# Two-layer encoder step on one core: the first feed-forward product as seven block products

## The chip, the core and the metric

The kernel runs on one core of one Trainium2 chip. The metric is the device time of one execution in microseconds (us). The five engines are named as the profile names them: PE (TensorE, matrix multiplication), DVE (VectorE), ACT (ScalarE), POOL (GpSimd) and SP (SyncE, which here only issues transfers).

## The reference

Two layers, each a token mixer and then a gated feed-forward part with a causal convolution of width 3. There are 656 token rows: 16 meta rows and 512 prompt rows of one stream, and 8 sample streams of 16 rows. The change touches the feed-forward part only:

```python
def conv_ffn(h, p, buf):
    u = h @ p['w_ffn_up']
    a, v = u[..., :D_FF], u[..., D_FF:]
    T = a.shape[1]
    ext = jnp.concatenate([buf.astype(a.dtype), a], axis=1)
    w = p['ffn_conv_w']
    c = p['ffn_conv_b'] + sum(ext[:, j:j + T] * w[j] for j in range(CONV_W))
    out = (jax.nn.silu(c) * v) @ p['w_ffn_down']
    return out, ext[:, -(CONV_W - 1):]
...
    h = rmsnorm(x, p['norm_ffn_pre'])
    f, buf = conv_ffn(h, p, conv_buf)
    x = x + rmsnorm(f, p['norm_ffn_post'])
```

Here `D_MODEL` = 1024 and `D_FF` = 2816, so `w_ffn_up` is 1024 x 5632 and `w_ffn_down` is 2816 x 1024.

## The kernel before

**Layout.** Everything is feature-major: an activation is 8 tiles of 128 features by `T` = 656 tokens, and a product is taken over two halves of `HALF` = 328 tokens, one half to a PSUM bank. Four PSUM tensors of two banks each (`G0`, `G1`, `WA`, `WB`) hold all products.

**Precision.** A product in float32 is made of three products in the type fp32r: each operand is split in a high part (ACT copies it, which rounds: `whi`, `Hh`, `gh`) and a rest (DVE subtracts: `wlo`, `Hl`, `gl`), and PE takes low x high, high x high and high x low. So a tile of 128 outputs over 8 tiles of inputs is 8 x 2 halves x 3 = 48 matmuls of 128 x 328.

**The stream of weights.** The weights come in pieces of 128 x 1024 through SP into a ring of two raw slots (`wraw`), are split by `w_high` (ACT, line 1156) and `w_low` (DVE, line 1723) into a ring of three slots (`whi`, `wlo`), and PE's `tile` (line 556) waits for the semaphore `w_split` of its piece. ACT waits for the tile that used the slot before.

**The feed-forward part of a layer.** The 22 chunks of 128 gate columns and 128 value columns are worked in two halves of 11. In a half, PE makes for each chunk a gate tile and a value tile (`tile`, called at line 1044 and after), 96 matmuls; then the down product of the half, 8 tiles of 11 chunks, 66 matmuls each. For each chunk DVE takes the gate tile out of PSUM times the norm factor `R` into `ax`, convolves it in three operations into `cc`, ACT takes the silu into `tmp`, DVE multiplies it by `R` and by the value tile, ACT copies the high part into `gh` and DVE subtracts the rest into `gl`. The down product of the first half is copied to `Y` by ACT, that of the second half added to it by DVE. The last three down tiles are worked by halves of the tokens (`last_tiles`, line 601), so that the norm behind them can begin on the first half, and the next layer begins with `first_two` (line 616), three tiles worked by halves as their inputs come.

**What sets the order.** There is no planner: each engine's program is written out by hand, works strictly in order, and waits on counting semaphores. DVE and ACT also wait for their own previous instruction. The helpers through which all instructions pass give their line to the profile: L513 for a matmul, L1642 for DVE, L1082 for ACT; so instructions are told apart by the names of their tiles. POOL's own work (`normalize`, `split_out`, `decay_state`) lies in the token mixer, and POOL has none in the feed-forward part.

## Time and profile before

| | |
|---|---|
| time, median of 3 executions | 1893.23 us (1892.51 to 1893.58) |
| span of the profiled execution | 1891.6 us |
| PE busy | 1851.7 us (98%), 12092 matmuls |
| PE weight loads | 1712.9 us (91%) |
| DVE busy | 1109.8 us (59%), 1803 instructions |
| ACT busy | 753.1 us (40%), 1221 instructions |
| POOL busy | 97.2 us (5%), 105 instructions |
| chain that ended last | PE 85%, DVE 7%, ACT 5% |

The span runs from the first to the last instruction of one profiled execution. No time of its own is given for that execution beside the span: the median of the timed executions lies 1.6 us above it. A busy share says how long an engine worked, not whether anybody waited for it; the chain of work that ended last says that. The granted clock of PE is full (0.9 or more) in each of the 40 slices of the span.

### The profile page before, as it was taken

Reading aid. Unit: us, or ns where it says so; the run is one execution under the profiler, and the core shown is the slowest. Engines: PE = TensorE matmul, PEld = TensorE weight load, DVE = VectorE, ACT = ScalarE, POOL = GpSimd, SP = SyncE. Lnnn points to the kernel's source line nnn. Section 1 sums busy time; section 2 is a strip of 40 time slices with the busy share of each in tenths; the row PEclk is TensorE's granted clock in tenths of the full one; section 3 lists DMA queues with packets and bytes.
Section 4 is the critical chain, followed back from the end, with each engine's and each line's share of the span. In section 5 each row is a group of like instructions: output and inputs, shape, how many; then the busy total and the mean of one; then the engine's idle time right before and its main releaser. Section 6 shows DMA issues by size and latency. Waiting matters only on the chain.

```text
span 1891.6 us, 30407 instructions
## 1 busy us (share of the span) xinstructions
PE 1851.7 (98%) x12092; PEld 1712.9 (91%) x12092; DVE 1109.8 (59%) x1803; ACT 753.1 (40%) x1221; POOL 97.2 (5%) x105
## 2 busy tenths in 40 slices
PE   8999999999999999999999999999999999999996
PEld 7999976598999999999999999657989999999995
DVE  5777875426766226654577778654377551466635
ACT  5444546435422222222564444554363222222234
POOL 0000023200000000000000000340000000000000
PEclk9999999999999999999999999999999999999999
DMA  5312121411222222222231122314112222122211
GB/s 179 95 58 69 63 74 55 158 41 49 80 80 69 78 67 68 79 78 74 65 109 47 58 69 73 80 55 130 56 49 91 77 75 71 67 79 78 68 67 62
DMA packets 46380, 143.83 MB, mean 76 GB/s; under 512 B 5952, under 2 KB 11968, under 8 KB 46216
## 3 DMA queue, kind: packets, MB, share of 16 engines
q1 hardware_dynamic: 38704, 124.12, 20.3%
q10 hardware_dynamic: 7536, 17.78, 2.7%
q8 instruction: 96, 1.57, 0.3%
q14 instruction: 44, 0.36, 0.1%
HBM read 130.80 MB, written 8.65 MB: 74 GB/s over the span
## 4 chain that ended last, share of the span: by engine, by line
PE 85%; DVE 7%; ACT 5%; issue 1%; DMA 1%; ACTq 0%; DVEq 0%; SPq 0%
PE G L513 68%; PE WA L513 10%; PE WB L513 5%; PE G L517 1%; DVE wlo L1642 1%; PE WB L517 1%; ACT sq L1082 1%; DVE DE L1642 1%; ACT R L1082 1%; DVE Z L1642 1%; DVE tmp L1642 1%; ACT Hh L1082 1%; DVE Y L1642 1%; DVE Hl L1642 1%; DMA wraw<-in_wstream 1%
## 5 line engine op out<-in xcount | busy, mean ns | idle before, releaser
L513 PE MATMUL G<-Hh,wlo 128*128 128x328 f32 x2144 | 688.5, 321 | 12.0 <-DVE Hl L1642 8.5
L513 PE MATMUL G<-Hh,whi 128*128 128x328 f32 x2144 | 673.2, 314 | 0.0
L513 PE MATMUL G<-Hl,whi 128*128 128x328 f32 x2144 | 667.8, 311 | 0.0
L513 PEld LDWEIGHTS G<-Hh,wlo 128*128 128x128 f32 x2144 | 404.7, 189 | 23.5 <-DVE Hl L1642 12.6
L513 PEld LDWEIGHTS G<-Hh,whi 128*128 128x128 f32 x2144 | 404.1, 188 | 2.2 <-issue 0.2
L513 PEld LDWEIGHTS G<-Hl,whi 128*128 128x128 f32 x2144 | 404.5, 189 | 0.0
L1082 ACT ACTIVATE whi<-wraw 128x1024 fp32r<-128x1024 f32 (+2 forms) x198 | 203.0, 1025 | 475.8 <-PE G L513 458.0
L1642 DVE TENSOR_TENSOR wlo<-wraw,whi 128x1024 fp32r<-128x1024 f32 (+2 forms) x198 | 234.1, 1182 | 224.7 <-ACT whi L1082 213.6
L513 PE MATMUL G<-gl,whi 128*128 128x328 f32 x628 | 196.6, 313 | 0.0
L513 PE MATMUL G<-gh,wlo 128*128 128x328 f32 x628 | 195.9, 312 | 0.0
L513 PE MATMUL G<-gh,whi 128*128 128x328 f32 x628 | 195.9, 312 | 0.0
L1642 DVE TENSOR_TENSOR ax<-G,R 128x328 f32<-128x328 f32 (+2 forms) x126 | 48.6, 386 | 136.5 <-PE G L513 133.2
L513 PEld LDWEIGHTS G<-gh,whi 128*128 128x128 f32 x628 | 118.0, 188 | 0.0
L513 PEld LDWEIGHTS G<-gh,wlo 128*128 128x128 f32 x628 | 117.9, 188 | 0.0
L513 PEld LDWEIGHTS G<-gl,whi 128*128 128x128 f32 x628 | 117.9, 188 | 0.0
L1082 ACT ACTIVATE tmp<-cc 128x528 f32<-128x528 f32 x88 | 42.1, 479 | 149.2 <-DVE cc L1642 147.8
L1642 DVE SCALAR_TENSOR_TENSOR cc<-ax,cols,cc 128x672 f32<-128x672 f32 x88 | 80.9, 919 | 3.1
L1082 ACT ACTIVATE DE<-DE 128x512 f32<-128x512 f32 (+2 forms) x64 | 43.3, 677 | 63.5 <-DVE DE L1642 59.2
L456 POOL TENSOR_TENSOR S<-S,dec 128x1024 f32<-128x1024 f32 x8 | 15.2, 1898 | 988.4 <-PE WA L513 988.4
L1642 DVE TENSOR_TENSOR DE<-Y 128x328 f32<-128x328 f32 (+4 forms) x128 | 57.9, 452 | 4.8
L513 PEld LDWEIGHTS WA<-Z 128*128 128x128 f32 (+3 forms) x544 | 48.8, 165 | 12.0 <-DVE Z L1642 6.7
L513 PE MATMUL WA<-sq,ones 128*128 128x328 f32 x144 | 52.2, 449 | 4.3 <-ACT sq L1082 4.3
(270 smaller groups left out, 2487.2 us busy)
## 6 DMA issues: line engine op xcount, KB each, us to landing
wraw<-in_wstream SPq DMA_DIRECT2D x192, 512.0 KB, 3.3
ckT<-in_ckT SPq DMA_DIRECT2D x12, 512.0 KB, 3.5
S<-in_s ACTq DMA_DIRECT2D x8, 512.0 KB, 6.1
o_sst<-S ACTq DMA_DIRECT2D x8, 512.0 KB, 2.9
ctok<-in_ctok SPq DMA_DIRECT2D x8, 512.0 KB, 3.6
o_y<-Y SPq DMA_DIRECT2D x16, 164.0 KB, 2.0
ckT<-in_ckT ACTq DMA_DIRECT2D x4, 512.0 KB, 3.9
ctok<-in_ctok ACTq DMA_DIRECT2D x4, 512.0 KB, 4.0
```

Of the source, the lines that this page charges most:

```text
L456: pool.tensor_tensor(s3, s3, dec[:, :].rearrange("p (b a) -> p b a", a=1).broadcast_to([P, DB, P]), ALU.mult).then_inc(S("s0_decayed"), 1)
L513: return pe.matmul(out, lhsT, rhs, start=start, stop=stop, skip_group_check=True)
L517: return pe.transpose(out, in_, ident[0:n, 0:n])
L1082: return act.activation(*args, **kw)
L1642: return kind(*args, **kw)
```

## The change

**Seven products instead of eight.** A chunk is seen as a 2 x 2 by 2 x 2 block product: its weights are four blocks (gate or value columns, first or second half of the 1024 inputs), its inputs four blocks (first or second half of the inputs, first or second half of the tokens). For the chunks 3 to 21 of each layer PE makes seven products of 4 input tiles x 3 = 12 matmuls each, 84 in all, in the order `B11, B21, T2, T3, T1, T4, B22`, in three PSUM banks; results that serve twice are copied or added between the products by ACT and DVE. The chunks 0 to 2 stay as they were ("plain"). PE's program has 9808 rows instead of 10264.

**Sums of inputs and weights.** Per layer POOL makes two differences of token halves, ACT and DVE make sums and their splits from them (`Sh`, `Sl`). Per chunk POOL makes four sums of blocks of weights, 128 x 512 each (`early_sums`: `T3`, `T1`, `T2`; `late_sum`: `T4`), into `t2`, `t3` and in place. Each of the seven blocks is split by ACT and DVE on its own, 128 x 512. Raw pieces have four slots (`wraw`, `wff`) from the pass of the first group on.

**Six passes of the down product.** The chunks are worked in groups of 2, 4, 4, 4, 4, 4; after each group a pass adds its share of the 8 down tiles. `gh` and `gl` shrink from 11 chunks to 4. ACT copies the first pass to `Y`, DVE adds the five others. `R` is multiplied once onto `Y` after the fifth pass, and per chunk in the last group only. The pieces of a pass come in parts of 128 to 512 columns.

**Smaller edits.** The first of the three operations of the convolution goes from DVE to ACT (`conv_first`), the other two work on `tmp` in two parts each. The last pass works the tiles 3 to 7 by halves, where before three tiles were. The convolution's state comes into `cout` with runs of 16 elements, where before it came into `cst` with runs of 352.

The core of the diff:

```diff
+GROUPS = [(0, 2), (2, 6), (6, 10), (10, 14), (14, 18), (18, KF)]
+B11, B21, T2, T3, T1, T4, B22 = range(PRODUCTS)
...
+            def early_sums(l, c):
...
+                if j:
+                    pool.wait_ge(S("w_split"), unit_of(j - 1, T3) + 1)
...
+                pool.tensor_tensor(t3[:, :], v[:, 0:W_HALF], v[:, W_HALF:W_PIECE], ALU.add).then_inc(S("T"), 1)
+                sum_wait(l, c, T3)
+                pool.tensor_tensor(v[:, 0:W_HALF], v[:, 0:W_HALF], w[:, 0:W_HALF], ALU.add).then_inc(S("T"), 1)
...
+                pool.tensor_tensor(t2[:, j % 2, :], v[:, 0:W_HALF], v[:, W_HALF:W_PIECE], ALU.add).then_inc(S("T"), 1)
+            def late_sum(l, c):
...
+                pool.wait_ge(S("w_split"), unit_of(j, B21) + 1)
...
+            def chunk(l, c):
...
+                product(B11, x_, Hh[:, lo, a_], Hl[:, lo, a_], True)
+                product(B21, y_, Hh[:, hi, a_], Hl[:, hi, a_], True)
...
+                pe.wait_ge(S("act_took"), act_took(l, c, 0))
+                product(T2, x_, Sh[:, 1, :, :], Sl[:, 1, :, :], False)
...
+                product(T3, z_, Sh[:, 2, :, :], Sl[:, 2, :, :], True)
...
+                pe.wait_ge(S("act_took"), act_took(l, c, 1))
+                product(T1, x_, Sh[:, 0, :, :], Sl[:, 0, :, :], False)
+                pe.wait_ge(S("act_took"), act_took(l, c, 2))
+                product(T4, z_, Hh[:, hi, b_], Hl[:, hi, b_], False)
...
+                pe.wait_ge(S("dve_took"), dve_took(l, c))
+                product(B22, x_, Hh[:, lo, b_], Hl[:, lo, b_], False)
...
+                for n in range(3):
+                    if q == 0 and n != 1:
+                        tt = l * TILES + T_UP + 4 + n // 2
+                        pe.wait_ge(S(f"evac{tt % 2}"), slot_use(tt))
...
+                    elif n != 1:
+                        pe.wait_ge(S("gl"), 2 * (l * KF + c1 - 2 + n // 2) + 1)
...
+                    blocks(n, 0, nk - 1)
+                for n in range(3):
+                    blocks(n, nk - 1, nk)
```

ACT's part of a chunk (`pending` is the chunk before):

```diff
+                def chunk(c, pending):
...
+                    if pending is not None:
+                        conv_first(pending)
+                    highs(l, u0 - 1)
+                    after(B11)
+                    act.wait_ge(S("conv"), 2 * (l * KF + c) - 1)
+                    did(f(p1, bank(G[s], 0), ACT.Copy), "act_took")
+                    highs(l, u0 + B11)
+                    if pending is not None:
+                        silu(pending)
+                    highs(l, u0 + B21)
+                    after(T2)
+                    did(f(u2, bank(G[s], 0), ACT.Copy), "act_took")
+                    highs(l, u0 + T2)
+                    after(T3)
+                    act.wait_ge(S("gl"), 2 * (l * KF + c) - 1)
+                    did(f(p7[:, :], bank(WA, s), ACT.Copy), "act_took")
+                    if pending is not None:
+                        g_high(pending)
```

**How the order moves on DVE.** Before, one chunk on DVE goes from one `gl` to the next. Most of it, in the first half of layer 0:

```order
L1642 TENSOR_TENSOR gl<-tmp,gh 128x656 [waits w_split,gh]
L1642 COPY ax<-cst 128x8x2 [waits gl]
L1642 TENSOR_TENSOR ax<-G0,R 128x328 [waits dve,tile]
L1642 TENSOR_TENSOR ax<-G0,R 128x200 [waits dve]
L1642 TENSOR_TENSOR ax<-G0,R 128x8x16 [waits dve]
L1642 COPY cout<-ax 128x2 [waits evac0]
L1642 COPY cout<-ax 128x16 [waits dve]
L1642 TENSOR_SCALAR cc<-ax,cols 128x672 [waits dve,silu]
L1642 SCALAR_TENSOR_TENSOR cc<-ax,cols,cc 128x672 [waits dve] x2
L1642 TENSOR_TENSOR wlo<-wraw,whi 128x1024 [waits conv,w_hi]
L1642 TENSOR_TENSOR tmp<-tmp,R 128x656 [waits w_split,silu]
L1642 TENSOR_TENSOR tmp<-G1,tmp 128x656 [waits dve,tile]
```

The change on DVE, second group of layer 0, from the end of its first chunk (6) into its second (7). `R2` and `p7` hold results between products, `ax` the gate rows, `tmp` the convolution:

```order
L2078 TENSOR_TENSOR R2<-R2,WA 128x328 [waits dve_took,product]
L2078 TENSOR_TENSOR ax<-R2,R 128x200 [waits dve]
L2078 TENSOR_TENSOR ax<-R2,R 128x8x16 [waits dve]
L2078 COPY cout<-ax 128x18 [waits dve]
L2078 SCALAR_TENSOR_TENSOR tmp<-ax,cols,tmp 128x528 [waits conv,silu]
L2078 SCALAR_TENSOR_TENSOR tmp<-ax,cols,tmp 128x128 [waits dve]
L2078 SCALAR_TENSOR_TENSOR tmp<-ax,cols,tmp 128x528 [waits dve]
L2078 SCALAR_TENSOR_TENSOR tmp<-ax,cols,tmp 128x128 [waits dve]
L2078 TENSOR_TENSOR wlo<-t2,whi 128x512 [waits conv,w_hi]
L2078 TENSOR_TENSOR wlo<-t3,whi 128x512 [waits w_split,w_hi]
L2078 COPY ax<-cout 128x8x2 [waits w_split]
L2078 TENSOR_TENSOR wlo<-wff,whi 128x512 [waits dve,w_hi]
```

and on, to the end of the chunk; the row after the last is again the first of the fence above:

```order
L2078 TENSOR_TENSOR ax<-G1,R2 128x328 [waits w_split,act_took,product]
L2078 TENSOR_TENSOR ax<-ax,R 128x328 [waits dve]
L2078 TENSOR_TENSOR wlo<-wff,whi 128x512 [waits dve,w_hi]
L2078 TENSOR_TENSOR wlo<-wff,whi 128x512 [waits w_split,w_hi]
L2078 SCALAR_TENSOR_TENSOR tmp<-G0,tmp 128x328 [waits w_split,product,silu]
L2078 SCALAR_TENSOR_TENSOR tmp<-p7,tmp 128x328 [waits dve]
L2078 TENSOR_TENSOR wlo<-wraw,whi 128x512 [waits gl,w_hi]
L2078 TENSOR_TENSOR gl<-tmp,gh 128x656 [waits w_split,gh]
L2078 TENSOR_TENSOR wlo<-wraw,whi 128x512 [waits gl,w_hi]
L2078 TENSOR_TENSOR p7<-p7,G1 128x328 [waits w_split,act_took,product]
```

So a chunk is 22 instructions now. The first convolution row waits for ACT's `conv_first`, which itself waits for the copy right ahead of it. Splits of the chunk after (`B11`, `B21`) stand ahead of the `p7` addition, for which PE's last product waits.

**POOL in a chunk** (layer 0, chunk 5; each waits for a split of DVE, and for its own semaphore `T`):

```order
L703 TENSOR_TENSOR t3<-wff 128x512 [waits w_split,w_in3,w_in2]
L705 TENSOR_TENSOR wff<-wff 128x512 [waits T]
L709 TENSOR_TENSOR t2<-wff 128x512 [waits w_split,T]
L716 TENSOR_TENSOR wff<-wff,t2 128x512 [waits T,w_split]
L703 TENSOR_TENSOR t3<-wraw 128x512 [waits w_split,w_in1,w_in0]
```

Before, no row of POOL stood in the feed-forward part.

**The first pass.** PE goes from the sixth plain tile straight into the first pass, whose tiles take the banks of `G0` (gate tile of chunk 2), `WB` and `G1` (value tile of chunk 2):

```order
L746 MATMUL G0<-gh,wlo 128x328 [waits gl,w_split,evac0]
L746 MATMUL G0<-gh,whi 128x328
L746 MATMUL G0<-gl,whi 128x328
L746 MATMUL G0<-gh,wlo 128x328 [waits w_split]
L746 MATMUL G0<-gh,whi 128x328
L746 MATMUL G0<-gl,whi 128x328
L746 MATMUL WB<-gh,wlo 128x328 [waits w_split,evac0]
L746 MATMUL WB<-gh,whi 128x328
L746 MATMUL WB<-gl,whi 128x328
L746 MATMUL WB<-gh,wlo 128x328 [waits w_split]
L746 MATMUL WB<-gh,whi 128x328
L746 MATMUL WB<-gl,whi 128x328
```

On DVE, what frees `G0` stands behind the sums and splits of the inputs, and what frees `G1` comes behind the last row shown:

```order
L2078 TENSOR_TENSOR Sl<-Y,Sh 128x1312 [waits s_dve,s_act]
L2078 COPY ax<-cout 128x8x2 [waits s_dve]
L2078 TENSOR_TENSOR ax<-G0,R 128x328 [waits dve,tile]
L2078 TENSOR_TENSOR ax<-G0,R 128x200 [waits dve]
L2078 TENSOR_TENSOR ax<-G0,R 128x8x16 [waits dve]
L2078 COPY cout<-ax 128x18 [waits evac0]
L2078 TENSOR_TENSOR wlo<-wraw,whi 128x1024 [waits conv,w_hi]
L2078 SCALAR_TENSOR_TENSOR tmp<-ax,cols,tmp 128x528 [waits w_split,silu]
L2078 SCALAR_TENSOR_TENSOR tmp<-ax,cols,tmp 128x128 [waits dve]
L2078 SCALAR_TENSOR_TENSOR tmp<-ax,cols,tmp 128x528 [waits dve]
L2078 SCALAR_TENSOR_TENSOR tmp<-ax,cols,tmp 128x128 [waits dve]
L2078 TENSOR_TENSOR Sl<-Y,Sh 128x1312 [waits conv,s_act]
```

The plain tiles before met no such rows: the next gate tile of `G0` waited only for the reads of the one before.

## Rows read from the trace of the kernel before

**Rows 1.** The page, its first lines: span, then busy time, share and instructions.

```profile
span 1891.6 us, 30407 instructions
...
PE 1851.7 (98%) x12092; PEld 1712.9 (91%) x12092; DVE 1109.8 (59%) x1803; ACT 753.1 (40%) x1221; POOL 97.2 (5%) x105
```

**Rows 2.** The chain of waits: start, length, what; first feed-forward product on, layer 0.

```profile
490.30 417.27 PE G L513 x2778
```

**Rows 3.** DVE's instructions by shape, whole run: line, operation, busy, mean ns | idle.

```profile
L1642 DVE SCALAR_TENSOR_TENSOR cc<-ax,cols,cc 128x672 f32<-128x672 f32 x88 | 80.9, 919 | 3.1
...
L1642 DVE TENSOR_TENSOR gl<-tmp,gh 128x656 fp32r<-128x656 f32 x44 | 37.1, 842 | 4.9 <-DVE wlo L1642 0.5
L1642 DVE SCALAR_TENSOR_TENSOR Hl<-X,cols,Hh 128x328 fp32r<-128x328 f32 x64 | 35.8, 560 | 23.6 <-ACT Hh L1082 19.1 <-DVEq L1642 0.2
...
L1642 DVE TENSOR_TENSOR ax<-G,R 128x328 f32<-128x328 f32 x42 | 21.0, 500 | 133.6 <-PE G L513 133.2
...
L1642 DVE TENSOR_TENSOR ax<-G,R 128x200 f32<-128x200 f32 x42 | 15.4, 366 | 1.4
...
L1642 DVE TENSOR_TENSOR ax<-G,R 128x128 f32<-128x128 f32 x42 | 12.2, 291 | 1.4
...
L1642 DVE SCALAR_TENSOR_TENSOR st<-st,DE,WA 128x128 f32<-128x128 f32 x32 | 11.1, 347 | 3.4
...
L1642 DVE COPY ax<-cst 128x16 f32<-128x16 f32 x44 | 7.7, 176 | 1.6
...
L1642 DVE TENSOR_TENSOR wlo<-wraw,whi 128x512 fp32r<-128x512 f32 x4 | 2.8, 693 | 0.4
```

**Rows 4.** DVE in order of time, layer 0: start, length, instruction.

```profile
495.81 1.23 DVE L1642 TENSOR_TENSOR wlo<-wraw,whi 128x1024 fp32r<-128x1024 f32 x1
497.13 0.84 DVE L1642 TENSOR_TENSOR tmp<-tmp,R 128x656 f32<-128x656 f32 x1
...
500.47 0.84 DVE L1642 TENSOR_TENSOR gl<-tmp,gh 128x656 fp32r<-128x656 f32 x1
501.35 0.18 DVE L1642 COPY ax<-cst 128x16 f32<-128x16 f32 x1
```

**Rows 5.** ACT's instructions by shape, whole run, the same columns.

```profile
L1082 ACT ACTIVATE gh<-tmp 128x656 fp32r<-128x656 f32 x44 | 33.2, 754 | 10.0 <-DVEq L1642 5.9 <-ACT whi L1082 0.7
L1082 ACT ACTIVATE tmp<-cc 128x528 f32<-128x528 f32 x44 | 28.5, 647 | 147.8 <-DVE cc L1642 147.8
...
L1082 ACT ACTIVATE tmp<-cc 128x128 f32<-128x128 f32 x44 | 13.7, 311 | 1.4
...
L1082 ACT ACTIVATE Y<-Y,lbs 128x656 f32<-128x656 f32 x8 | 7.5, 937 | 0.1
...
L1082 ACT ACTIVATE sq<-G 128x328 f32<-128x328 f32 x8 | 3.6, 445 | 10.8 <-PE G L513 10.3
```

**Rows 6.** POOL in order of time, layer 0, just before the output projection.

```profile
337.29 1.57 POOL L477 TENSOR_TENSOR Hl<-ob,Hh 128x656 fp32r<-128x656 f32 x1
338.82 1.28 POOL L474 TENSOR_TENSOR Hh<-ob,zero 128x656 fp32r<-128x656 f32 x1
```

**Rows 7.** DVE in order of time, in the same stretch.

```profile
337.43 1.45 DVE L1642 TENSOR_TENSOR ms<-ms 128x1 f32<-128x1 f32 x1
...
339.11 1.55 DVE L1642 TENSOR_SCALAR Ps<-Ps,ms 128x1040 f32<-128x1040 f32 x1
```

**Rows 8.** DVE's instructions by shape, whole run: the second form of rows 7.

```profile
L1642 DVE TENSOR_SCALAR Ps<-Ps,ms 128x1040 f32<-128x1040 f32 x16 | 13.8, 860 | 0.6
```

**Rows 9.** DVE and PE in order of time, first feed-forward product begins, layer 0.

```profile
481.65 1.23 DVE L1642 TENSOR_TENSOR ax<-G,R 128x328 f32<-128x328 f32 x3
...
490.30 0.39 PE L513 MATMUL G<-Hh,wlo 128*128 128x328 f32 x1 [0.70 <-DVE wlo L1642]
```

**Rows 10.** DVE in order of time, end of layer 0.

```profile
922.97 0.50 DVE L1642 TENSOR_TENSOR Y<-Y,G 128x328 f32<-128x328 f32 x1 [3.87 <-PE G L513]
...
962.73 0.56 DVE L1642 SCALAR_TENSOR_TENSOR Hl<-X,cols,Hh 128x328 fp32r<-128x328 f32 x1 [1.06 <-ACT Hh L1082]
```

More of the change, by code:

```diff
@@ L295, in build @@
+        split_after = {}
+        _i = P_UP + 2 * NPL - 1
+        for _u in range(U_PROD[NPL], UNITS_L):
+            _w, _k = max(users[UNITS_L + _u]) - UNITS_L, product_of(_u)
+            if _k and product_of(_w):
+                _w += LATE[_k[1]]
+            _i = max(_i, _w)
+            split_after.setdefault(_i, []).append(_u)
         UNITS = [(h, j) for h in range(HM) for j in range(4)]
@@ L576, in tile @@
                         m.then_inc(S("tile"), 1)
-                    if c + P == W_PIECE and len(chunks) == FH and not last:
-                        m.then_inc(S("w_mid"), 1)
                     if after is not None:
@@ L597, in half_tile, with last_tiles @@
                         m.then_inc(S(done), 1)
-                    if x and c + P == W_PIECE and len(chunks) == FH and not last:
-                        m.then_inc(S("w_mid"), 1)
-            def last_tiles(tt, chunks, rh, rl, done, whole=0):
+            def last_tiles(tt, chunks, rh, rl, done):
                 n = len(chunks[0])
@@ new lines, in _ @@
+                act.wait_ge(S("hl"), (l + 1) * SPLITS)
+                for k in range(KH):
+                    step(f(Y[:, KH + k, cols_of(1)], X[:, k, cols_of(1)], ACT.Copy, scale=cols[:, l, C_FFNPRE + k:C_FFNPRE + k + 1]))
+                conv_first(0)
+                act.wait_ge(S("d"), 2 * l + 1)
+                for k in range(KH):
+                    did(f(Y[:, k, cols_of(0)], Y[:, k, cols_of(0)], ACT.Copy, scale=cols[:, l, C_FFNPRE + k:C_FFNPRE + k + 1]), "s_act")
+                silu(0)
@@ new lines, in _ @@
+                for q, (c0, c1) in enumerate(GROUPS):
+                    for c in range(max(c0, NPL), c1):
+                        chunk(c, c - 1 if c > max(c0, NPL) else None)
+                    last_c, u0, nk = max(c1 - 1, NPL - 1), U_PASS[q], c1 - c0
+                    if q:
+                        conv_first(last_c)
+                        highs(l, u0 - 1)
+                        silu(last_c)
+                    else:
+                        highs(l, u0 - 1)
+                        act.wait_ge(S("tile"), t0 + T_UP + 2 * NPL)
+                        s_high(Hh[:, 0:KH, cols_of(1)], 8, 1, 0)
+                    g_high(last_c)
+                    for n in range(KD):
+                        if not q:
+                            act.wait_ge(S("down"), down_no(l, q, n))
+                            act.wait_ge(S("s_dve"), s_split(l, 1 if n < KH else 3))
+                            did(f(two(Y[:, n, :]), halves(down_bank(n)), ACT.Copy), "act_took")
+                        if q < NQ - 1 and nk * (n + 1) % 8 == 0:
+                            highs(l, u0 + nk * (n + 1) // 8 - 1)
@@ L1515, in _ @@
+                split_to[0] = 0
+                for n in range(3):
+                    act.wait_ge(S("dve_took"), down_added(l, NQ - 1, n))
+                    square_x(n0 + N_FFNPOST, n, Y[:, n, :])
+                    step(f(Y[:, n, :], Y[:, n, :], ACT.Copy, scale=cols[:, l, C_FFNPOST + n:C_FFNPOST + n + 1]))
                 exp_table()
@@ new lines, in _, with ffn_out_b @@
+                split_to[0] = 0
+                for n in range(3, KD):
+                    dve.wait_ge(S("half_a"), AH * l + n + 1)
+                    did(tt_(Y[:, n, cols_of(0)], Y[:, n, cols_of(0)], bank(half_bank(n, 0), 0), ALU.add), "y2")
+                    if n > 3:
+                        add_square_a(n0 + N_FFNPOST, n - 1, AH * l + n)
+                add_square_a(n0 + N_FFNPOST, KD - 1, AH * (l + 1))
+                def ffn_out_b(n):
+                    dve.wait_ge(S("down"), down_no(l, NQ - 1, n))
+                    did(tt_(Y[:, n, cols_of(1)], Y[:, n, cols_of(1)], bank(half_bank(n, 1), 1), ALU.add), "y2")
```

757 lines of the change are left out of this document (548 added, 209 removed).

## The prediction

> **What bounds the kernel now.** I read the page first: PE is busy for 1851.7 of 1891.6 us, DVE for 1109.8, POOL for 97.2 [rows 1]. Then the chain of waits: in layer 0, from the fifth feed-forward tile to nearly the end of the down product, it is one piece of 417.27 us on PE with 2778 matmuls and nothing between them [rows 2]. That is 0.1502 us a matmul. So every matmul taken out there is worth 0.150 us, and every microsecond in which PE must wait costs a full one. Last I read the groups by shape and the order of time on DVE, ACT and POOL, for what they have to do beside a shorter chunk.
>
> **What is removed.** 19 chunks in each of 2 layers lose 12 of 96 matmuls: 456, as PE's 10264 rows become 9808. 456 x 0.1502 = **-68.5 us**. The down product keeps its count. A chunk falls on PE from 14.4 us to 84 x 0.1502 = 12.6 us.
>
> **DVE in a chunk.** A chunk is 22 rows of DVE: seven splits of 512 columns at 0.693 = 4.85; four convolution operations, two of 528 columns at 0.77 (on the line from 0.560 for 328 to 0.919 for 672) and two of 128 at 0.347, 2.23; six operations of 328 columns at 0.500 = 3.0; 0.366 and 0.291; `gl` 0.842; two small copies at 0.176 [rows 3]. Together 11.9 us. The gaps come on top: 0.10 where another engine is also waited for (497.13 against 497.04), 0.04 where only DVE's own semaphore is (501.35 against 501.31) [rows 4]. With 13 of the one and 9 of the other: 1.7 us. That alone is 13.6 us against PE's 12.6.
>
> **Two trips to ACT in DVE's way.** `conv_first` stands between two neighbouring rows of DVE. On ACT its parts are the widths 528 and 128, which take 0.647 and 0.311 without pointer operands; a scale and a bias by pointer make 656 columns 0.937 instead of 0.754 [rows 5], so I add 0.18 to each: 1.3 us, and 1.4 with the handovers, while DVE stands. Second, ACT may copy `p7` only after DVE's `times_v` of the chunk before, and `gh` comes behind that: 0.445 + 0.754 + handovers = 1.3 us [rows 5], of which a split hides 0.8. Together 1.9 us. The cycle of a middle chunk is thus 11.9 + 1.7 + 1.9 = **15.5 us**, and it is DVE's: PE waits about 0.8 us ahead of `T2` and 2.1 us ahead of `T4` and `B22`, because `p7`'s addition stands behind splits of the next chunk. The chunk before took 14.4 us.
>
> **By groups.** The first chunk of a group finds its splits made during the pass: 12.6 us. I laid the rows of both engines behind each other for the others: 15.6, 15.5, and 16.1 for the last, where ACT's trip is bare and a down piece of 1.23 us is split. Then the pass waits 0.65 us for `times_v` of the last chunk, since its third tile takes that bank. A group of four takes 60.5 us, not 4 x 12.6 = 50.4: +10.1. The group with three new chunks: 44.9, not 37.8: +7.1. The last has 0.94 us more per chunk for the multiplication by `R` (0.842 and a gap) [rows 3]: +13.8. Per layer 7.1 + 3 x 10.1 + 13.8 = 51; two layers **+102 us**. The passes themselves (28.8 us for 192 matmuls) hide DVE's additions, eight of 0.84 us.
>
> **POOL against DVE.** POOL's four sums need 512 columns of two inputs; its operation of that kind on 656 took 1.57 [rows 6], by width 1.23 each. Do they cost DVE anything? While POOL worked from 337.29 to 338.86 and from 338.82 to 340.10, DVE's one-column operation, begun at 337.43, took 1.45 us, and the scaling begun at 339.11 took 1.55 [rows 6, 7], where its mean is 0.860 [rows 8]. Each lasts until shortly before the POOL operation is over. I take it that the two engines exclude each other. The Trainium skill ("SBUF — State Buffer", Who interferes with whom) says so: a DVE instruction with two SBUF inputs contends with a GpSimd instruction that reads SBUF, and whoever is second fully blocks. By that rule the sum is the one below, and without it the second rival's; this case's trace agrees with it in the two places named. Laid into the middle chunk, `T3` is released by a split and blocks the next split for 1.0 us, `T1` falls on an addition from PSUM and costs 0.4, `T2` 1.0, and `T4` meets two additions from PSUM: 2.4 us. It falls in the chunks with a successor in the group, except the first of each group: 1 + 4 x 2 = 9 per layer, 18 x 2.4 = **+43 us**. Bounds: 0, and 4 x 1.1 x 18 = 79.
>
> **The passage to the new form.** From the first `ax` row at 481.65 [rows 9] I add DVE's rows: ACT has four scaled copies ahead of `conv_first` and four more behind it, DVE sums 12 tiles (0.56 each) and makes four splits of 1312 columns (1.53 each, on the line of rows 3). The split for the fifth plain tile is ready at 492.4 instead of 490.3 [rows 9]; the gate tile of chunk 2 leaves `G0` at 511.9, while PE has been ready for the first pass since 506.9 (492.4 and two tiles of 7.2); the value tile leaves `G1` at 518.5, with 1.8 us of matmuls between. PE waits 2.1 + 5.0 + 4.8 = 12 us a layer: **+24 us**. Bounds 12 and 32, the latter if POOL's two sums of 1312 columns also block the halo copy.
>
> **The end of a layer.** Behind the last first half of the down tiles 96 matmuls (14.4 us) stood as cover, now 60 (9.0 us). The norm, the residual and the splits of the next layer took DVE from 922.97 to 963.29 [rows 10]. At the end of layer 0 I take 5 us of the 5.4 as lost; at the end of layer 1 the second half decides, so 0 to 1: **+5 us**. Bounds 0 and 12.
>
> **Sum.** -68.5 + 102 + 43 + 24 + 5 = +105.5. The profiled execution's span is 1891.6; the sum gives a span of 1997, and with the 1.6 us by which the median lies above it **1999 us**.
>
> **Rivals.**
> - *DVE keeps up (faster).* If the holes close, because gaps overlap with what I take as waits and PE finds every bank free, the chunks cost 12.6 us: 1893.2 - 68.5 = 1825, and with the passage and the end 1854. It decides where the cycle of a middle chunk is under about 13.6 us: then the excess per layer is under 20 us and the sum negative. For it speaks only that DVE is at 59% over the whole run [rows 1]; against it that 11.9 us of bare durations leave 0.7 for 22 gaps and two trips to ACT. Chance 0.10.
> - *No exclusion in most places.* The two engines overlap with little loss, as they may when POOL's requests fall in the holes: 1999 - 43 = 1956. For it: DVE stands 1.9 us in each cycle. Against it: the sums are released by a split of DVE, right where the next one follows. Chance 0.24.
> - *POOL becomes the chain.* It is blocked by DVE as well as blocking it; then `T2`'s sum comes late for ACT's copy and the cycle grows by another 1 to 2 us in 18 chunks, and in the last chunks too: 2020 to 2040. Against it: 1 us of slack between the third sum and ACT's copy. Chance 0.13.
> - *Even:* losses of just 68 us, chance 0.03.
>
> **How the numbers follow.** The forecast has 0.50: 1999, its own range 1970 to 2020. With the second and third rival the range reaches from 1930 to 2040; the first lies below it, and part of the tails, together under 2 in 10. A measurement of this kernel tells 0.2% (3.8 us) from no change. Faster by more than that 0.10, within it 0.03, slower 0.87.
>
> **What would show it.** Right: PE's matmuls about 456 fewer, at 0.150 us each as before; PE idle in the feed-forward parts, released by DVE `p7`, `wlo` and ACT; middle chunks 15.5 us apart or more; waits near 5 us ahead of the first pass; DVE busy over 85% there; splits on DVE whose mean is well over 0.693 us, and POOL sums over 1.23, where they meet. Wrong: PE without gaps over the chunks; a cycle near 12.6; splits at their old mean beside POOL's sums, which would leave only the second rival.

## The result, and the profile after

The changed kernel takes **2032.7 us** in the median (2030.6 to 2035.2), the kernel before 1893.3: a ratio of **1.074** (95% interval 1.073 to 1.076). The forecast was 1999 us; its own range was 1970 to 2020, and 1930 to 2040 with the rivals. So the measured time lies outside the forecast's own range and inside the wider one. The profiled execution has a span of 2033.4 us against 1891.6, 141.8 more.

The page's head and its chain line, then the waits of PE over the whole run (in all, times, longest, us):

```profile
span 2033.4 us, 31440 instructions
PE 1854.6 (91%) x11636; PEld 1691.3 (83%) x11636; DVE 1367.1 (67%) x2229; ACT 962.6 (47%) x1601; POOL 324.4 (16%) x261
PEclk9999999999899999998899999999989999999988
...
PE 57%; DVE 28%; ACT 10%; issue 3%; DVEq 0%; DMA 0%; ACTq 0%; SPq 0%
```

```profile
PE WA L746 <- ACT p L1431: 55.7, 27, 3.7
PE G L746 <- DVE wlo L2078: 27.9, 24, 4.1
PE G L746 <- DVE p L2078: 20.3, 18, 1.6
PE G L746 <- DVE tmp L2078: 19.5, 12, 3.0
PE G L746 <- DVE ax L2078: 10.2, 2, 5.1
PE WA L746 <- DVE acc L2078: 9.2, 5, 8.0
PE G L746 <- DVE Hl L2078: 8.8, 3, 8.1
```

PE has 456 matmuls less and is yet busy for 1854.6 us, where it was busy for 1851.7 [rows 1]. Its idle time went from 39.9 to 178.8 us, +138.9. Its busy time should have fallen by 68.5 and rose by 2.9: +71.4 us. -68.5 + 138.9 + 71.4 = 141.8. Some 50 of the 71.4 us are 402 matmuls that began while the granted clock was at the lower of its two levels, 1.2 and not 2.4 GHz: they follow each other in 0.275 us and not 0.150. Most of the rest comes from how busy time is counted: the last matmul of every unbroken piece counts in full, 0.31 us instead of 0.15, and there are 142 pieces where there were 62. The page shows slices with much of the lower clock as 8s in its row `PEclk` (a 9 is 0.9 or more), and the clock's record has 27 stretches of 3.4 to 11.1 us, 147.6 us together, most of them begun during a wait of PE for another engine or just behind one (before: 3 stretches, 15.5 us). This split by PE's time says how PE spent the run, not what set its length. For that, the middle of a chunk as DVE saw it (start, duration, what; in brackets the idle time ahead and who ended it), and POOL beside it:

```profile
719.96 0.17 DVE L2078 COPY cout<-ax 128x18 f32<-128x18 f32 x1
721.55 2.35 DVE L2078 SCALAR_TENSOR_TENSOR tmp<-ax,cols,tmp 128x528 f32<-128x528 f32 x4 [1.43 <-ACT tmp L1431]
...
725.81 1.69 DVE L2078 TENSOR_TENSOR wlo<-wff,whi 128x512 fp32r<-128x512 f32 x1
727.63 0.50 DVE L2078 TENSOR_TENSOR ax<-G,R 128x328 f32<-128x328 f32 x1
728.16 0.85 DVE L2078 TENSOR_TENSOR ax<-ax,R 128x328 f32<-128x328 f32 x1
729.12 2.39 DVE L2078 TENSOR_TENSOR wlo<-wff,whi 128x512 fp32r<-128x512 f32 x2
...
734.11 0.84 DVE L2078 TENSOR_TENSOR gl<-tmp,gh 128x656 fp32r<-128x656 f32 x1 [0.63 <-ACT gh L1431]
735.05 0.69 DVE L2078 TENSOR_TENSOR wlo<-wraw,whi 128x512 fp32r<-128x512 f32 x1
735.88 0.50 DVE L2078 TENSOR_TENSOR p<-p,G 128x328 f32<-128x328 f32 x1
736.48 0.49 DVE L2078 TENSOR_TENSOR R<-R,WA 128x328 f32<-128x328 f32 x1
737.00 0.69 DVE L2078 TENSOR_TENSOR ax<-R 128x200 f32<-128x200 f32 x2
737.73 0.17 DVE L2078 COPY cout<-ax 128x18 f32<-128x18 f32 x1
```

```profile
725.67 1.28 POOL L703 TENSOR_TENSOR t<-wraw 128x512 f32<-128x512 f32 x1 [9.10 <-DVE wlo L2078]
727.03 1.63 POOL L705 TENSOR_TENSOR wraw<-wraw 128x512 f32<-128x512 f32 x1
728.73 1.43 POOL L709 TENSOR_TENSOR t<-wraw 128x512 f32<-128x512 f32 x1
735.82 1.27 POOL L716 TENSOR_TENSOR wraw<-wraw,t 128x512 f32<-128x512 f32 x1 [5.66 <-DVE wlo L2078]
```

From one carry copy to the next DVE takes 737.73 - 719.96 = **17.77 us**, of which it stands 1.43 and 0.63 for ACT. A split of 512 columns bare takes 0.69; the one that begins 0.14 us behind POOL's first sum takes 1.69, and the pair that meets the third takes 2.39 in the place of 2 x 0.69. `ax<-G,R`, which reads one of its inputs from PSUM, keeps its 0.50 beside the second sum; `ax<-ax,R`, with both in SBUF, goes to 0.85. The fourth sum begins behind a split and meets additions with one input from PSUM, and costs nothing. PE's 12.6 us of matmuls have no part in this loop. From carry copy to carry copy the other middle chunks take 17.8 to 18.3 us (18.7 to 19.2 in the last groups, with `R`).

Where the 141.8 us went, by place. For each stretch between PE's first matmul of a group or a pass and the next such one, I took the time and subtracted 0.1502 us for each matmul in it. The first line is a count times 0.1502, and no time of its own.

| Place | forecast | measured |
|---|---|---|
| matmuls taken out | -68.5 | -68.5 |
| chunks in groups, and the passes between | +102 + 43 = +145 | +149.1 |
| passage to the new form | +24 | +37.1 |
| ends of the layers | +5 | +29.0 |
| waits of before in these stretches, and parts that the change leaves alone | 0 | -4.9 |
| sum | +105.5 | +141.8 |

A group of four takes 64.5 to 65.6 us in its chunks (the last, with `R`, 67.9 and 68.0), where 50.4 would be bare. Of the 149.1 us the chunks have 137 (139 by the forecast), and the eight passes between groups 12.

### The profile page after: what moved, and what is told of

It is laid out like the page before. It is cut to its first block, busy times and chain, and to the rows that moved or that the text cites. A ratio compares the mean times of both kernels' runs of the same rounds, so it can differ in the third digit from the quotient of the medians.

```text
span 2033.4 us, 31440 instructions
## 1 busy us (share of the span) xinstructions
PE 1854.6 (91%) x11636; PEld 1691.3 (83%) x11636; DVE 1367.1 (67%) x2229; ACT 962.6 (47%) x1601; POOL 324.4 (16%) x261
## 4 chain that ended last, share of the span: by engine, by line
PE 57%; DVE 28%; ACT 10%; issue 3%; DVEq 0%; DMA 0%; ACTq 0%; SPq 0%
PE G L746 34%; PE WA L746 13%; DVE wlo L2078 8%; PE WB L746 8%; DVE tmp L2078 7%; DVE ax L2078 3%; ACT tmp L1431 3%; DVE Y L2078 2%; ACT sq L1431 1%; PE G L750 1%; DVE gl L2078 1%; DVE R L2078 1%; ACT Y L1431 1%; PE WB L750 1%; ACT R L1431 1%
## 5 line engine op out<-in xcount | busy, mean ns | idle before, releaser
L746 PE MATMUL G<-Hh,wlo 128*128 128x328 f32 x1384 | 462.2, 334 | 44.2 <-DVE p L2078 20.3
L746 PE MATMUL G<-Hh,whi 128*128 128x328 f32 x1384 | 442.2, 320 | 0.0
L746 PE MATMUL G<-Hl,whi 128*128 128x328 f32 x1384 | 441.2, 319 | 0.0
L746 PEld LDWEIGHTS G<-Hh,wlo 128*128 128x128 f32 x1384 | 270.3, 195 | 62.3 <-DVE p L2078 26.1
L746 PEld LDWEIGHTS G<-Hh,whi 128*128 128x128 f32 x1384 | 270.1, 195 | 2.3 <-issue 0.4
L746 PEld LDWEIGHTS G<-Hl,whi 128*128 128x128 f32 x1384 | 268.5, 194 | 0.0
L2078 DVE SCALAR_TENSOR_TENSOR tmp<-ax,cols,tmp 128x528 f32<-128x528 f32 (+1 forms) x176 | 98.6, 560 | 49.3 <-ACT tmp L1431 43.2
L746 PE MATMUL WA<-Hh,wlo 128*128 128x328 f32 x216 | 77.3, 358 | 55.7 <-ACT p L1431 55.7
L2078 DVE TENSOR_TENSOR wlo<-wff,whi 128x512 fp32r<-128x512 f32 (+1 forms) x118 | 106.5, 902 | 27.2 <-ACT whi L1431 16.1
L746 PE MATMUL G<-Sh,wlo 128*128 128x328 f32 x304 | 96.7, 318 | 13.3 <-DVE wlo L2078 13.3
L746 PE MATMUL G<-Sl,whi 128*128 128x328 f32 x304 | 95.0, 313 | 0.0
```

Source lines behind the costliest of these rows:

```text
L746: return pe.matmul(out, lhsT, rhs, start=start, stop=stop, skip_group_check=True)
L2078: return kind(*args, **kw)
```

## The experiments

Each time is the median on the chip, with its ratio to the kernel before and the interval. The changed kernel to compare with is 2032.7, 1.0742 (1.0727 to 1.0757). The kernel before, timed beside each group of runs, had medians of 1892.8 to 1893.6 us, so the times can be compared with each other. Stretches "by place" are those of the table above.

**1. What POOL's sums cost DVE.** Two kernels keep the waits and take the width, or the reading, away. All sums of a chunk are changed in the same way; the first of them:

```diff
-                pool.tensor_tensor(t3[:, :], v[:, 0:W_HALF], v[:, W_HALF:W_PIECE], ALU.add).then_inc(S("T"), 1)
+                pool.tensor_tensor(t3[:, 0:1], v[:, 0:1], v[:, 1:2], ALU.add).then_inc(S("T"), 1)
```

> POOL's four sums of weights per chunk shrink to one column each, with the same waits around them; the splits of T2, T3, T1 and T4 read unsummed blocks, so these four products are of the wrong weights, and everything else is computed. Theory (DVE's own loop sets the pace of the chunks, and POOL's sums block it for 2.4 us in each middle chunk): the cycle of a middle chunk falls from 17.8 to 15.5 us, 18 x 2.35 = 42 us less, about 1990 us. Rival 1 (the sums cost nothing, the rest of the loop is 18 us by itself): 2033 us. Rival 2 (the lower granted clock is what makes the chunks long): 2033 to 2025, and the stretches of lower clock stay as many.

```diff
+                pool.memset(t3[:, :], 0.0).then_inc(S("T"), 1)
```

> As the run before, but in place of each sum POOL fills the same 128 x 512 tile with a constant: a write of the full width that reads nothing. The four products are of unsummed weights. If it is POOL's reading that shuts DVE out: splits at 0.69 us beside it and the same time as with one column, about 1990 us. If any POOL operation of that width does it: as the changed kernel, 2033 less what the fill is shorter.

One column: **1980.4 us**, 1.0465 (1.0447 to 1.0482). Constants of full width: **1978.5**, 1.0458 (1.0439 to 1.0477). DVE's splits of 512 columns in the changed kernel, then in the second of these, and POOL's operations in the latter (x count, then busy and mean ns; there are more splits of `wff` in it, since those of `t` now read `wff` too):

```profile
L2078 DVE TENSOR_TENSOR wlo<-wff,whi 128x512 fp32r<-128x512 f32 x100 | 84.4, 844 | 24.1 <-ACT whi L1431 14.3 <-DVE ax L2078 0.5 <-DVEq L2078 0.3
L2078 DVE TENSOR_TENSOR wlo<-wraw,whi 128x512 fp32r<-128x512 f32 x94 | 84.1, 895 | 10.3 <-ACT whi L1431 0.8
```

```profile
L2078 DVE TENSOR_TENSOR wlo<-wff,whi 128x512 fp32r<-128x512 f32 x140 | 97.0, 693 | 37.7 <-ACT whi L1431 23.5 <-DVE wlo L2078 0.5 <-DVE ax L2078 0.5
...
L703 POOL MEMSET t<- 128x512 f32 x38 | 20.0, 527 | 450.9 <-DVE wlo L2078 223.4 <-DMA wraw<-in_wstream 182.2 <-issue 45.3
```

The splits are back at 0.693 us beside a POOL that writes just as wide a tile but reads nothing. The fill is shorter than a sum, but it does run while a split does (in one chunk from 716.23 to 716.76 us, the split from 716.40), and the split keeps its 0.69. So it is the reading that shuts DVE out. The Trainium skill ("SBUF — State Buffer", Who interferes with whom) names exactly this pair, a DVE instruction with two SBUF inputs and a GpSimd instruction that reads SBUF, and exempts one that only writes; both runs agree. In the run with one column a group of four takes 12.6, 15.8, 15.5 and 16.1 us, 60.0 in all, and over the chunks of the ten groups 42.4 us are gone, where I had expected 42. DVE's loop is 15.5 us in all 14 middle chunks of the groups without `R`. The spans differ by 54.7 us: by place 5.5 more are gone in the passage, where the sums of chunk 3 were, 5.4 at the ends of the layers and 2.6 in the passes. The stretches of lower clock fell from 27 to 12, against the rival that made them the cause of long chunks; but that they go together does not yet say which causes which, and experiment 4 does.

**2. Less work on DVE.** Three of four operations of the convolution left out:

```diff
-                    for i in (1, 2):
+                    for i in (2,):
                         w = col(l, C_CW + i * KF + c)
-                        step(stt(d[:, 0:PT], s_[:, i:i + PT], w, d[:, 0:PT], ALU.mult, ALU.add))
```

> Three of the four DVE operations of the convolution in a chunk are left out (both of the second tap, the prompt part of the third): two of 528 columns at 0.78 us, one of 128 at 0.35, with gaps 2.05 us of DVE. Theory (DVE's loop): 28 chunks have them between two chunks of a group, 28 x 2.05 = 57 us less, about 1975 us; up to 4 us more if the passes feel it. Rival (PE and ACT's chain over p7 sets the pace, DVE has slack): within 5 us of 2033.

**1955.7 us**, 1.0329 (1.0312 to 1.0346): 77 us less, 20 more than the chunks' own count gives. Groups of four fell to 58.5 to 59.0, 6.2 us each for 6.2 us of operations taken out; the rest came from the passes (11 us), the passage (6) and the ends (5), where DVE is also what PE waits for. The rival, a chain over `p7` with DVE in slack, falls.

**3. A second `p7`.** The longest entry of PE's waits, 55.7 us for ACT's copy of `p7`, invites to take it for the bound.

```diff
+        def p7_of(c):
+            return p7b[:, :] if (GROUPS[group_of(c)][1] - 1 - c) % 2 else p7[:, :]
...
-                    act.wait_ge(S("gl"), 2 * (l * KF + c) - 1)
-                    did(f(p7[:, :], bank(WA, s), ACT.Copy), "act_took")
+                    act.wait_ge(S("gl"), 2 * (l * KF + c) - 3)
+                    did(f(p7_of(c), bank(WA, s), ACT.Copy), "act_took")
```

> A second buffer for p7, used in turns, so ACT's copy behind T3 waits for the chunk before last. Everything is computed. Theory (DVE's loop): PE's wait ahead of T4 (27 of them, 55.7 us) goes, and comes back ahead of B22 and T2, because the addition to p7 and the splits still stand in DVE's order; only the 0.63 us in which DVE waits for gh can close: 28 x 0.6 = 17 at most, 2016 to 2033 us. Rival (the single buffer's chain is the bound): the 55.7 us go, about 1978 us.

**2016.4 us**, 1.0653 (1.0637 to 1.0668): 16.3 less. PE's waits in that run:

```profile
PE G L750 <- DVE p L2082: 35.4, 16, 3.9
PE G L750 <- DVE p7b L2082: 30.1, 10, 3.9
```

The wait for ACT is gone, and 65.5 us for DVE's additions stand in its place, where 20.3 stood. What was won shows on DVE, in the time for which it stood for `gh` (changed kernel, then this one):

```profile
L2078 DVE TENSOR_TENSOR gl<-tmp,gh 128x656 fp32r<-128x656 f32 x44 | 40.5, 920 | 34.3 <-ACT gh L1431 33.7
```

```profile
L2082 DVE TENSOR_TENSOR gl<-tmp,gh 128x656 fp32r<-128x656 f32 x44 | 39.5, 897 | 19.9 <-ACT gh L1435 17.4
```

33.7 - 17.4 = 16.3 us, as much as the gain; DVE's idle time of every kind ahead of `gl` fell by a little less, 14.4 us, so that the two numbers agree to the tenth is chance. A wait's size in the list is no measure of what its removal brings.

**4. The granted clock.** Useless matmuls keep PE at work in its waits ahead of `T4` (PE also waits, ahead of them, until the pass before has freed their bank):

```diff
+                def spare(n):
+                    for _ in range(n):
+                        mm(bank(WB, 0), Sh[:, 0, 0, 0:P], Sh[:, 1, 0, :])
...
                 product(T1, x_, Sh[:, 0, :, :], Sl[:, 0, :, :], False)
+                if not first:
...
+                    spare(4 if c + 1 == GROUPS[q][1] else 20)
```

> PE works matmuls of no use into WB, which no chunk uses, between T1 and T4: 20 in the 18 chunks that are neither first nor last of their group, 4 in the 10 last ones; 400 x 0.15 = 60 us of PE laid into waits of 3.6 and about 1 us. Everything is computed. Theory (DVE's loop sets the chunks; a lower granted clock there slows matmuls that have room): the stretches of lower clock inside the chunks go, of 147.6 us at least 50, and the time falls by 2 to 8 us only, since a group of four takes 64.5 to 65.6 us where DVE's loop alone gives 64.7. Rival (the lower clock makes the chunks long): 36 us of slowed matmuls in the chunks go, about 1997 us.

**2036.5 us**, 1.0753 (1.0736 to 1.0771): no gain, and the 4 us more are within the uncertainty. The stretch from the first new chunk to the last of layer 0, changed kernel first (us of each engine, x count; then `PEclk`):

```profile
536.00:960.00 424.00, 376.03 (x2347) 365.73 (x2346) 295.92 (x460) 176.71 (x276) 97.27 (x70) 0.96 0.21 67
```

```profile
536.00:960.00 424.00, 394.21 (x2551) 384.55 (x2549) 295.92 (x460) 176.49 (x276) 98.06 (x71) 1.00 0.21 66
```

The clock is at its upper level throughout, 2551 matmuls fit where 2347 did, and DVE does the same 460 instructions in the same 295.92 us. By place the chunks and passes take 1.6 us less than in the changed kernel (147.5 above bare, not 149.1). The lower clock is a symptom in the chunks: it slows matmuls that would otherwise have waited. My own expectation, 2 to 8 us less, was already too much. The run leaves the passage and the ends of the layers as they were, and says nothing about the clock there.

**5. The first operation of the convolution back on DVE** (and ACT's part left out).

```diff
-                    dve.wait_ge(S("silu"), 2 * (l * KF + c) + 1)
...
+                    w, b = col(l, C_CW + c), col(l, C_CB + c)
+                    step(ts(d[:, 0:PT], s_[:, 0:PT], w, b, ALU.mult, ALU.add))
+                    step(ts(dv, sv[:, :, 0:DT], w, b, ALU.mult, ALU.add))
```

> The first operation of the convolution goes back from ACT to DVE, in two parts of 528 and 128 columns; everything is computed. The profile of before has that kind with 672 columns at 0.63 us, so some 0.50 and 0.20 us and two gaps of 0.04 come in the place of DVE's hole of 1.43 us: theory (the loop through DVE counts the trip to ACT as it counts work): 0.7 us less in each of 28 chunks, and little in the passes, 2010 to 2015 us. Rival (work on DVE is what counts, the hole is covered by PE's slack): 28 x 0.8 more, 2055 us.

**2047.9 us**, 1.0817 (1.0798 to 1.0835): 15 slower, a miss. The chunks did what was expected in direction: a group of four fell by 1.5 us on average, to 63.3 to 63.7. By place the chunks are 12.8 us shorter in all. But the eight passes between groups grew from 30.3 to 32.8 us in the mean, 19.6 us in all, the passage by 3 and the ends by 3. The start of one pass, in this run:

```profile
773.52 1.23 DVE L2072 TENSOR_TENSOR wlo<-wraw,whi 128x1024 fp32r<-128x1024 f32 x1
774.78 0.94 DVE L2072 TENSOR_SCALAR tmp<-ax,cols 128x528 f32<-128x528 f32 x2
775.75 2.35 DVE L2072 SCALAR_TENSOR_TENSOR tmp<-ax,cols,tmp 128x528 f32<-128x528 f32 x4
778.20 2.34 DVE L2072 TENSOR_TENSOR wlo<-wff,whi 128x1024 fp32r<-128x1024 f32 x1
```

There a split of 1024 columns had covered ACT's trip whole, so 0.94 us of work came on top; and what followed moved under one of POOL's sums: 2.34 us for a split that takes 1.23. PE's wait for `tmp` in this pass went from 1.0 to 2.7 us. I had counted the passes at nothing.

**6. The order in the passage.** The gate tile of chunk 2 is evacuated ahead of four sums and a split of 1312 columns, the value tile ahead of another split:

```diff
+                plain_a(2)
+                w_low(l, P_UP + 7)
                 for k in range(KH):
...
+                conv_rest(2)
                 s_low(1, Sl[:, 2, :, :], Sh[:, 2, :, :], 0, 0)
-                plain_a(2)
-                w_low(l, P_UP + 7)
-                conv_rest(2)
+                plain_v(2)
                 s_low(2, Sl[:, 0, :, :], Sh[:, 0, :, :], 1, 1)
-                plain_v(2)
```

> In the passage to the new form DVE evacuates the gate tile of chunk 2 ahead of the third four sums and the second split of 1312 columns, the value tile ahead of the third split, and ACT does silu ahead of Sh's third part. Everything is computed. Theory (PE's waits of 5.0 and 2.9 us ahead of the first pass are DVE's order, and the lower clock follows from them): 4 to 6 us less per layer, 2021 to 2025 us in all. Rival (T2 or T3 of chunk 3 then waits for Sl instead): 2030 us or more, with a new wait of PE for Sl.

**2031.3 us**, 1.0728 (1.0712 to 1.0744), 1.4 less and within the uncertainty: another miss. PE's waits from 478 to 545 us in this run:

```profile
PE G L746 <- DVE tmp L2078: 6.9, 1, 6.9
PE G L746 <- DVE wlo L2078: 4.0, 1, 4.0
PE G L746 <- DVE ax L2078: 1.2, 1, 1.2
```

The wait for the gate tile (`ax`) fell from 5.0 to 1.2, and that for the value tile (`tmp`) rose from 2.9 to 6.9. Together the three waits are 12 us as before. The value tile's evacuation was hardly earlier, since nearly all of DVE's work still stood ahead of it. By place the two passages are 3.3 us shorter and the chunks and passes 2.0 longer. So this order did not help; with less DVE work, in `less_conv`, the passages are 6.4 us shorter (30.7 above bare, not 37.1).

**7. The end of the layer, from both sides.** In the changed kernel, DVE's last norm additions ahead of six residual additions:

```diff
-            residual(0, 2, 2)
             ffn_out_b(KD - 3)
-            residual(0, 4, 2)
             ffn_out_b(KD - 2)
...
+            residual(0, 2)
...
+            residual(0, 3)
+            residual(0, 4, 2)
             residual(0, 6, 2)
```

> At the end of layer 1 DVE works the last three tiles' second halves and their squares ahead of six of the eight residual additions of the first half. Everything is computed. PE's wait of 8.0 us for the norm's sum should fall to about 3 us; as DVE has the same rows to do behind it and only 2.6 us of its own waiting there can close, theory: 2 to 4 us less, 2029 to 2031 us. Rival (the norm's sum alone sets the end): 5 us less, 2027 us.

**2030.9 us**, 1.0729 (1.0713 to 1.0745): 1.8 less, just short of what was expected and within the uncertainty, so the median decides nothing. The profiled execution shows more at the place itself: PE's wait for the norm's sum fell from 8.0 to 3.2 us, and the end of layer 1 lies 8.8 us above the kernel before, where the changed kernel has 14.8 (12.6 to 14.0 in `passage`, `two_p7`, `hole` and `fill`, which leave this end alone). And the kernel *before*, with its cover cut to that of the changed one:

```diff
+                if whole:
+                    half_tile(tt, chunks[0], rh, rl, 1, (whole, n), "tile")
+                    half_tile(tt + 1, chunks[1], rh, rl, 1, (0, 8), None)
+                    norm_sum_a(done, WA)
+                    half_tile(tt + 1, chunks[1], rh, rl, 1, (8, n), "tile")
+                    half_tile(tt + 2, chunks[2], rh, rl, 1, (0, n), "tile")
+                    return
```

> The kernel before, with one edit: PE makes the norm's sum of the first half 39 matmuls later at both layer ends, so that 42 matmuls are left behind it, as in the changed kernel, and not 81. Nothing else differs; everything is computed. Theory (the residual additions, 10 us of DVE behind this sum, need the matmuls as cover; 39 x 0.15 = 5.9 us of it are gone): 5 to 6 us more at the end of layer 1 and 3 to 5 at that of layer 0, about 1903 us; this would be a third of the 29 us that the ends of the layers cost in the changed kernel. Rival (DVE's late additions in the last pass make these 29 us, the cover does not matter): within 2 us of 1893.

**1906.3 us**, 1.0063 (1.0049 to 1.0077): **12.7 us** for one instruction moved by 39 matmuls, twice; I had expected 8 to 11. By place it is 6.1 us at the end of layer 0 and 6.3 at that of layer 1. PE's first sum of the norm's second half in this run, and then, from the changed kernel, its first sum of the first half and that of the second:

```profile
1880.26 1.46 PE L513 MATMUL WA<-acc,ones 128*128 128x328 f32 x2 [5.64 <-DVE acc L1649]
```

```profile
1991.76 0.82 PE L746 MATMUL WA<-acc,ones 128*128 128x328 f32 x2 [0.40 <-DVE acc L2078]
...
2007.99 1.46 PE L746 MATMUL WA<-acc,ones 128*128 128x328 f32 x2 [7.99 <-DVE acc L2078]
```

In the unchanged kernel that wait was 0.58 us. Behind the first half's sum DVE has some 10 us of work, 7.1 us of it residual additions, ahead of the last of the second half's squares; it no longer fits under the matmuls that are left.

**8. The same sums, where DVE does not read.** T2's sum is taken from `t3`, so that T1's can come last, in DVE's hole:

```diff
-                pool.tensor_tensor(t2[:, j % 2, :], v[:, 0:W_HALF], v[:, W_HALF:W_PIECE], ALU.add).then_inc(S("T"), 1)
+                pool.tensor_tensor(t2[:, j % 2, :], t3[:, :], w[:, 0:W_HALF], ALU.add).then_inc(S("T"), 1)
...
+                pool.wait_ge(S("conv"), 2 * (l * KF + c) - 1)
+                pool.tensor_tensor(v[:, 0:W_HALF], v[:, 0:W_HALF], w[:, 0:W_HALF], ALU.add).then_inc(S("T"), 1)
```

> POOL's sum for T2 is taken as t3 + the first block, so the sum for T1 needs no longer stand ahead of it; POOL makes T1's sum last, when DVE has passed the carry copy and waits 1.43 us for ACT's part of the convolution. The number and widths of the sums are the same; everything is computed. Theory (it is not POOL's work but its meeting with DVE's splits that costs): one of the two splits that are blocked for 1.0 us is free, T2's sum falls where T1's was (0.35 us on an addition), 18 x 1.0 = 18 us less, about 2015 us, with splits of wff and wraw nearer 0.69 us. Rival 1 (POOL's total time matters wherever it lies): 2033 us. Rival 2 (T1's split then comes late for T1): slower than 2033, with a wait of PE ahead of T1.

**2012.4 us**, 1.0637 (1.0620 to 1.0653): 20 less, with the same four sums. DVE's rows and POOL's moved sum in the chunk shown above:

```profile
725.99 1.70 DVE L2080 TENSOR_TENSOR wlo<-wff,whi 128x512 fp32r<-128x512 f32 x1
...
729.30 1.49 DVE L2080 TENSOR_TENSOR wlo<-wff,whi 128x512 fp32r<-128x512 f32 x2
...
738.61 2.35 DVE L2080 SCALAR_TENSOR_TENSOR tmp<-ax,cols,tmp 128x528 f32<-128x528 f32 x4 [1.43 <-ACT tmp L1433]
```

```profile
737.33 1.30 POOL L718 TENSOR_TENSOR wraw<-wraw 128x512 f32<-128x512 f32 x1 [0.96 <-DVE cout L2080]
```

The pair is 1.49 where it was 2.39, and the moved sum lies in the 1.43 us for which DVE stands anyway. One of the two blocked splits (1.70) is left.

**9. All reliefs at once, and the best that computes everything.** `relieved` has the edits of `sums_one_col`, `less_conv` and `two_p7`; `combined` those of `two_p7`, `hole` and `end`.

> Three reliefs of DVE's loop at once: POOL's sums of one column, three of the four operations of the convolution left out, two buffers for p7. The products T1 to T4 are of unsummed weights and the convolution lacks two taps; PE has all its matmuls. Theory: the loop falls from 17.8 to 17.8 - 2.35 - 2.05 - 0.6 = 12.8 us, so a group of four takes 51 to 54 us where it took 65, about 8 x 8 us less than with one column alone: 1905 to 1920 us. That would leave the change above the 1893 us of before even with DVE out of the way, by what the passage, the ends of the layers and the passes cost. Rival (another loop of 15 us or more, over ACT, stands behind DVE's): 1945 us or more.

> Two buffers for p7, T1's sum in DVE's hole, and the order at the end of layer 1; everything is computed. Theory: the gains add, 2033 - 16 - 18 - 2 = about 1997 us. Rival (with p7's wait gone DVE's hole moves and T1's sum meets a split again): 2005 to 2015 us.

`relieved`: **1893.2 us**, 1.0004 (0.9994 to 1.0014), 12 below the expectation's lower end. A group of four is 12.6, 13.3, 13.0 and 13.5 us, 52.4, near the 50.4 that PE needs. DVE's loop still sets it (13.0 us from one carry copy to the next, with no wait for PE in it), but it costs next to nothing, and there is still nothing won. By the same count as in the table, what the 68.5 us now pay for is 23 in the groups (10 of it in the two last ones, with `R`), 25 in the passages and 24 at the ends; 4 come back elsewhere, as in the table's last line. My expectation had counted only the chunks: the passages are 12 us shorter too, the passes 12 and the ends 5.

`combined`: **1995.2 us**, 1.0542 (1.0526 to 1.0558), as forecast by adding: 37.5 us less than the changed kernel. No version here is faster than the kernel before.

## Why the prediction was right, and where it was not

- **Removed matmuls:** 11636 rows on PE where 12092 were [rows 1], 456 less, at 0.150 us where the clock is up. Right.
- **The range:** 2032.7 is 13 us above the forecast's own range, 1970 to 2020. It lies below 2040 only because the range was widened for the rival "POOL becomes the chain", and that rival is not what happened (see below). That the time fell within the full range is luck; the direction and the two largest terms are not: DVE's cycle and POOL's sums were forecast at 145 us together, and 149 were measured.
- **DVE's cycle:** 15.5 us without POOL, and in `sums_one_col` DVE's loop takes 15.5. As PE sees it, that run has 15.8, 15.5 and 16.1 for the second, third and last chunk of a group, where the forecast had 15.6, 15.5 and 16.1. The hole at `conv_first` (1.43 for 1.4) and the wait for `gh` (0.63 for 0.5) are there. `less_conv` and `fill` show from both sides that DVE sets this pace and PE has room in it. DVE is busy for 14.2 of the 17.8 us of the middle chunk shown, 80% and not the 85% that the prediction named as a sign: the holds lengthen its instructions, but the two trips to ACT and the gaps stay. PE's wait ahead of `T4` was taken too small for one chunk (3.7, not 2.1), which changes nothing, since it is DVE's loop seen from PE. The passes were said to hide DVE's additions; the eight of them are 12 us above bare, where 5 stood (0.65 each).
- **POOL against DVE:** 2.4 us in each middle chunk forecast, 17.77 - 15.5 = 2.3 measured, and by the run 42.4 us where 43 stood. The single sum took longer than the 1.23 us that I had scaled from 656 columns: 1.27 to 1.63. The rival "no exclusion" (1956 us) falls by the runs of experiment 1, the rival "POOL becomes the chain" by the middle chunks, 17.8 to 18.3 us where it wanted 18.9 to 19.9, and by the waits of PE and ACT, none of which is for POOL. One of the two places from which the prediction read the exclusion is not a case of the rule that it cites: the scaling of `Ps` (1.55 us) reads one tile and a column of factors, not two tiles. And in both places it is the time for which DVE is held, not DVE's whole instruction, that ends shortly before POOL's: the scaling itself ends at 340.66, POOL's operation at 340.10.
- **The passage, +24, measured +37:** the waits of PE are 4.0, 5.0 and 2.9 us, 12 together, as forecast (2.1, 5.0 and 4.8), but two of the three are off and cancel by chance. The gate tile of chunk 2 left `G0` 3.5 us later than laid out (515.4, not 511.9), and the value tile `G1` with it (first matmul behind it at 521.95, not 518.5). Three of DVE's rows were held by POOL: the halo copy for 1.8 us (1.94 and not 0.18, in both layers), beside the second of POOL's sums of 1312 columns, and then, beside the sums for chunk 3, which I had not laid beside DVE's rows here, `gl` (1.75, not 0.84) and four sums of inputs (4.16, not 2.35).

```profile
478.99 4.01 POOL L686 TENSOR_TENSOR Y<-X 128x1312 f32<-128x1312 f32 x1
481.09 1.94 DVE L2078 COPY ax<-cout 128x16 f32<-128x16 f32 x1
...
505.39 1.86 POOL L703 TENSOR_TENSOR t<-wff 128x512 f32<-128x512 f32 x1 [22.39 <-issue]
...
506.20 1.75 DVE L2078 TENSOR_TENSOR gl<-tmp,gh 128x656 fp32r<-128x656 f32 x1
507.98 4.16 DVE L2078 SCALAR_TENSOR_TENSOR Y<-X,cols,Y 128x328 f32<-128x328 f32 x4
...
521.95 0.42 PE L746 MATMUL G<-gh,wlo 128*128 128x328 f32 x1 [2.94 <-DVE tmp L2078]
```

  Without the sums of chunk 3 at full width (`sums_one_col`) the passage was 2.7 us shorter per layer. And the 84 matmuls behind the last wait took 14.3 us, not 12.6, partly at the lower clock: 1.7 us per layer, one place where the clock does lie on the path. The step that failed is this term's size. It had the hold of the halo copy in its upper bound alone, though it did occur, and it left out the sums of chunk 3 and the lower clock. So even the bound of 32 was passed.
- **The end of a layer, +5, measured +29:** this is the step that was wrong in kind. It charged the matmuls that no longer stand as cover (5.4 us), once, for layer 0, and let "the second half decide" at the end of layer 1. In fact 10 us of DVE's work, residual additions above all, hang on the first half's sum and then delay the second half's; in the kernel before, cutting the cover alone costs 12.7 us, 6.1 at layer 0, where 5 stood, and 6.3 at layer 1, where 0 to 1 stood. The other 16 were not separated by a run, and their cause stays open; that the last pass begins with a wait for `times_v` of 2.6 us, and that the matmuls behind it and behind the norm run at the lower clock, is in the trace.
- **The clock:** no term, and some 50 us of slowed matmuls. It did not hurt the sum by that much, as `fill` shows: where DVE sets the pace, PE's slowness replaces its waiting.

So the mechanism of two thirds of the loss was right to a few us. The 36 us by which the sum fell short are 13 in the passage, 24 at the ends of the layers and 4 in chunks and passes, less 5 that came back elsewhere; both edges of the stretch were bounded too tightly (32 and 12, measured 37 and 29).

## What to carry to other kernels

Sum the engine that has to feed the shorter loop, with gaps, trips and exclusions, before counting what the fast engine saves: 12 matmuls less per chunk only moved the bound to DVE. An operation moved to an idle engine is free only where it does not shut another one out, as POOL's reading sums did with DVE; place it where the other stands anyway. Before shortening what lies at a stage's end, ask which dependent work had been hidden under it: 39 matmuls of cover less at each of two layer ends cost as much as 84 removed matmuls bring. And a range that is widened for a rival can hold the result when the rival does not: compare the parts of the sum, not only its total.
